# Expert weights through two rings of 11 places in one queue, and three bodies of an expert pass instead of four

## The reference, cut to what matters

```python
def swiglu(h, w1, w3, w2):
    return (jax.nn.silu(h @ w1) * (h @ w3)) @ w2

def moe_swiglu(h, router, w1, w3, w2):
    logits = (h @ router).astype(jnp.float32)
    top_v, top_i = lax.top_k(logits, TOP_K)          # TOP_K = 2 of 8
    probs = jax.nn.softmax(top_v, axis=-1)
    gate = jnp.sum(jax.nn.one_hot(top_i, N_EXPERTS, dtype=jnp.float32) * probs[..., None], axis=-2)
    out = jnp.zeros(h.shape, jnp.float32)
    for e in range(N_EXPERTS):
        out = out + gate[..., e:e + 1] * swiglu(h, w1[e], w3[e], w2[e]).astype(jnp.float32)
    return out.astype(h.dtype)
```

## Time and profile before

| What | Value |
|---|---|
| median of 3 runs | 2491.76 us |
| the profiled execution | 2489.43 us, its span 2487.6 us |
| TensorE busy (PE) | 2423.0 us, 97% |
| TensorE's weight load (PEld) | 2013.6 us, 81% |
| VectorE busy (DVE) | 1280.5 us, 51% |
| ScalarE busy (ACT) | 606.9 us, 24% |
| moved by DMA | 500.52 MB, 201 GB/s over the span |

### The profile page before, as it was taken

The page is one execution under the profiler, slowest core; times in us unless marked ns, Lnnn a source line. Parts: engine busy times, 40 slices in busy tenths (PEclk is TensorE's granted clock), DMA queues, the critical chain, the costliest instruction groups (busy, mean ns, idle before and its releaser), DMA issues. The chain is left out here.

```text
span 2487.6 us, 105448 instructions
## 1 busy us (share of the span) xinstructions
PE 2423.0 (97%) x46610; PEld 2013.6 (81%) x46610; DVE 1280.5 (51%) x3333; ACT 606.9 (24%) x1798; POOL 0.2 (0%) x4
## 2 busy tenths in 40 slices
PE   9999999999999999999999999999999999999998
PEld 7987666666699999898766666679899989888887
DVE  7666666666687676756665666668311111111111
ACT  2234333433311100223333334321111111111111
POOL 0000000000000000000000000000000000000000
PEclk9999999999999999999999999999999999999999
DMA  6334432222243443333343222234799999999997
GB/s 251 129 138 146 165 121 88 84 84 80 101 154 133 157 165 138 133 134 137 137 162 129 82 77 84 84 105 152 300 363 397 383 371 407 400 381 408 387 392 309
DMA packets 146068, 500.52 MB, mean 201 GB/s; under 512 B 18784, under 2 KB 23520, under 8 KB 143360
## 3 DMA queue, kind: packets, MB, share of 16 engines
q1 hardware_dynamic: 145792, 496.44, 53.5%
HBM read 476.08 MB, written 20.29 MB: 200 GB/s over the span
## 5 line engine op out<-in xcount | busy, mean ns | idle before, releaser
L302 PE MATMUL psum<-hT,ring 128*64 128x144 f32 (+1 forms) x4568 | 458.5, 346 | 3.4 <-DVE hT L2430 1.7
L455 PE MATMUL psum<-work,ring 128*64 128x88 f32 (+3 forms) x11264 | 417.6, 232 | 16.2 <-issue 5.8
L455 PEld LDWEIGHTS psum<-work,ring 128*64 128x64 f32 x11264 | 399.3, 136 | 35.4 <-issue 30.1
L302 PEld LDWEIGHTS psum<-hT,ring 128*64 128x64 f32 x4568 | 294.4, 137 | 95.0 <-issue 11.3
L2966 DVE TENSOR_TENSOR work<-psum,work 128x88 f32<-128x88 f32 (+3 forms) x176 | 42.4, 241 | 362.7 <-PE psum L455 362.5
L2667 PE MATMUL psum<-work,proj 128*64 128x88 f32 (+3 forms) x5632 | 203.5, 232 | 6.1 <-issue 4.5
L2667 PEld LDWEIGHTS psum<-work,proj 128*64 128x64 f32 x5632 | 196.8, 136 | 12.6 <-issue 9.6
L1776 ACT ACTIVATE work<-psum 128x256 f32<-128x256 f32 (+4 forms) x320 | 103.9, 362 | 349.9 <-PE psum L1687 84.8
L302 PE MATMUL psum<-work 128*64 128x144 f32 (+4 forms) x2096 | 155.4, 283 | 4.3 <-DVE work L1267 3.6
L302 PE MATMUL psum<-y_ret,work 128*64 128x144 f32 x2400 | 156.2, 286 | 0.8 <-DVE y_ret L532 0.8
L302 PEld LDWEIGHTS psum<-y_ret,work 128*64 128x64 f32 x2400 | 148.6, 137 | 1.0 <-issue 1.0
(11 more groups left out here) (518 smaller groups left out, 3695.7 us busy)
## 6 DMA issues: line engine op xcount, KB each, us to landing
ring<-w_ff_dram SPq DMA_DIRECT2D x424, 512.0 KB, 7.4
ring<-w_mix_dram SPq DMA_DIRECT2D x256, 512.0 KB, 3.8
proj<-w_ff_dram SPq DMA_DIRECT2D x128, 512.0 KB, 5.5
proj<-w_ff_dram SPq DMA_DIRECT2D x64, 384.0 KB, 5.8
work<-s_gla_dram SPq DMA_DIRECT2D x8, 1024.0 KB, 4.9
gla_s_out<-work SPq DMA_DIRECT2D x8, 1024.0 KB, 4.7
work<-s_ret_dram SPq DMA_DIRECT2D x8, 512.0 KB, 5.1
ret_s_out<-work SPq DMA_DIRECT2D x8, 512.0 KB, 2.7
```

What stands on the lines that cost most here:

```text
L302: last = nc.tensor.matmul(out[64 * c:64 * c + 64], weights[:, 64 * c:64 * c + 64], x, start=start, stop=stop)
L455: mm = nc.tensor.matmul(out[64 * c:64 * c + 64], ring[:, s, k, 64 * c:64 * c + 64], rhs[:, k0 + k, :], start=(k0 + k == 0), stop=(k0 + k = ...
```

## The change

The number of slots by rank becomes 88, 88, 80, 80, 80, 80, 72, 72: one class of four passes of 80 takes the place of 80, 80, 76, 76, and the bodies are three.

The weights get two rings of 11 places, for up and for down slabs. They use buffers that are free during the experts: up slabs lie in `lora_w` (2), `hT` (2), `y_ret` (2) and places 0 to 4 of `ring`; down slabs in `proj` (6), places 5 to 7 of `ring` and `merged` (2). Down weights are packed without gaps into 22 full slabs of 512 KB, so a slab runs across the border of two output tiles; a pass has 66 slabs of one size. SP's order is all 44 up slabs and then all 22 down slabs of each pass, each waiting for the slab 11 places earlier in its ring. Nothing is fetched behind the last pass. Of the 11 down places two pairs (4 and 5, 9 and 10) share a semaphore, and TensorE waits for both slabs of such a pair ahead of the first.

The first 22 slabs of the first pass are issued in `mix_out`, as the buffers come free between the join's pairs. TensorE's loops become 4 turns of 11 up slabs and 2 turns of 4 output tiles. Six banks take turns instead of four, and one count, `up_used`, that VectorE raises by 2 for each pair of slabs, replaces the two counts by which `up` waited; slab n waits until the pair that ends at slab n - 3 or n - 4 has been multiplied.

The diff, cut to its core:

```diff
-CLASSES = ((0, 2, 88), (2, 2, 80), (4, 2, 76))
+CLASSES = ((0, 2, 88), (2, 4, 80))
+EX_RING = 11
+EX_DOWN = D // 128 * FT // KT
+EX_SLABS = UP_SLABS + EX_DOWN
+UP_TURNS, DOWN_TURNS = UP_SLABS // EX_RING, EX_DOWN // EX_RING
...
+    up_slot = (slabs_in(lora_w[:, :, :], 2) + slabs_in(hT[:, :, :], 2) + slabs_in(y_ret[:, :, :], 2)
+               + [ring[:, i] for i in range(5)])
+    down_slot = slabs_in(proj[:, :, :], 6) + [ring[:, i] for i in range(5, RING)] + slabs_in(merged[:, :, :], 2)
+    DOWN_SHARED = {4: 5, 9: 10}
...
 (mix_out, SP, layer 1)
-                for j in range(RING):
-                    load_ff_slab(sp, 1, j, j, FF0 + j - RING + 1)
+                load_group(sp, S_RW_OUT, 1, 0, 4)
+                sp.wait_ge(slab_done, join_done(0))
+                up_ahead(0, 1)
+                load_group(sp, S_RW_OUT, 1, 4)
+                sp.wait_ge(slab_done, join_done(JOIN_GATES - 1))
+                up_ahead(2, 3, 4, 5)
+                load_first_group(sp, S_OUT)
+                sp.wait_ge(slab_done, join_done(OUT0 - 1))
+                down_ahead(0, 1, 2, 3, 4, 5)
+                for q in range(OUT0, OUT0 + 3):
+                    sp.wait_ge(slab_done, join_done(q))
+                    if q < OUT0 + 2:
+                        up_ahead(6 + 2 * (q - OUT0), 7 + 2 * (q - OUT0))
+                up_ahead(10)
+                down_ahead(6)
+                sp.wait_ge(slab_done, join_done(JOIN_PAIRS - 1))
+                down_ahead(7, 8, 9, 10)
...
 (experts, SP)
             def load_up(p, e, n):
-                load_ff_slab(sp, e, n, n % RING, freed_up(p, n))
+                sp.wait_ge(slab_done, count(p, EX_SLABS, FF0 + n - EX_RING + 1 - (EX_DOWN if n < EX_RING else 0)))
+                sp.dma_start(up_slot[n % EX_RING], w_ff[e, n]).then_inc(up_in[n % EX_RING], 16)
...
             with sp.Fori(0, after_first) as i:
-                for d in range(DRING):
-                    load_down(p, e, d)
-                for n in range(RING, UP_SLABS):
-                    load_up(p, e, n)
-                load_following(i, following, 2)
-                for d in range(DRING, DOWN_SLABS):
-                    load_down(p, e, d)
+                e = sp.value_load(ctl[0:1, bass.ds(i, 1)], min_val=0, max_val=NE)
+                for n in range(UP_SLABS):
+                    load_up((i, 1), e, n)
+                for d in range(EX_DOWN):
+                    load_down((i, 1), e, d)
...
 (experts, TensorE)
+                pe.wait_ge(up_in[s], turn * 16 + count(p, UP_TURNS * 16, earlier * 16 + 16))
+                pe.wait_ge(sig("up_used"), turn * EX_RING + count(p, UP_SLABS, GRANTED + s - 3))
...
-                with pe.Fori(0, UP_SLABS // RING) as g:
-                    for n in range(RING):
-                        up(p, cap, n, g)
-                for n in range(UP_SLABS // RING * RING, UP_SLABS):
-                    up(p, cap, n, 0)
+                with pe.Fori(0, UP_TURNS) as g:
+                    for s in range(EX_RING):
+                        up(p, cap, s, g)
...
-                with pe.Fori(0, KT // 2) as t:
-                    for m in range(2):
+                with pe.Fori(0, DOWN_TURNS) as t:
+                    for m in range(0, KT // DOWN_TURNS, 2):
                         down(p, cap, t, m)
...
 (host: the packing of the down weights)
-        for c in range(3):
-            n = 6 if c == 2 else 8
-            w_ff[e, UP_SLABS + c::3, :, 0:n] = s2[:, :, 8 * c:8 * c + n]
+        w_ff[e, UP_SLABS:EX_SLABS] = s2.transpose(0, 2, 1, 3).reshape(EX_DOWN, KT, 128, 128).transpose(0, 2, 1, 3)
```

More of the change, by code:

```diff
@@ L2166, in _, with up_ahead, down_ahead @@
         def _(sp):
-            load_group(sp, S_RW_OUT, 1)
-            load_first_group(sp, S_OUT)
+            def up_ahead(*slots):
+                for s in slots:
+                    sp.dma_start(up_slot[s], w_ff[1, s]).then_inc(up_in[s], 16)
+            def down_ahead(*slots):
+                for s in slots:
+                    sp.dma_start(down_slot[s], w_ff[1, UP_SLABS + s]).then_inc(down_in[s], 16)
             if dense:
+                load_group(sp, S_RW_OUT, 1)
+                load_first_group(sp, S_OUT)
                 for j in range(FF_SLABS):
@@ L2552, in _ @@
+                sp.dma_start(down_slot[d % EX_RING], w_ff[e, UP_SLABS + d]).then_inc(down_in[d % EX_RING], 16)
+            for n in range(EX_RING, UP_SLABS):
+                load_up((0, 0), 1, n)
+            for d in range(EX_RING, EX_DOWN):
+                load_down((0, 0), 1, d)
+            sp.wait_ge(sig("ctl"), 1)
             after_first = sp.value_load(ctl[0:1, ENTRIES + 1:ENTRIES + 2], min_val=NE - 1, max_val=FIXED - 1 + MAXR)
             with sp.Fori(0, after_first) as i:
-                e = expert_of(bass.ds(i, 1))
@@ L2567, in _ @@
             sp.wait_ge(sig("stored"), 4 * 16)
-            for s in range(RING):
-                per = len(range(s, UP_SLABS, RING))
-                fill = fills_before(layer, s) + fills(len(STREAM), s) + FIXED * per + 1
-                sp.wait_ge(slab_in[s], rest * (per * 16) + fill * 16)
-                settle(sp)
         @block.tensor
@@ L2655, in scatter_matrix, with down_here @@
                 last.then_inc(sig("scatter_ps"), 1)
+            def down_here(p, s, t):
+                both = 2 if s in DOWN_SHARED else 1
+                earlier = mixed_fills(s - 1) if 6 <= s < 9 else 0
+                pe.wait_ge(down_in[s], t * (both * 16) + count(p, DOWN_TURNS * both * 16, (earlier + both) * 16))
             def down(p, cap, t, m):
-                i, done = p
-                pe.wait_ge(sig("oT"), t * 2 + count(p, KT, m + 1))
-                for c in range(3):
-                    d = 3 * m + c
-                    pe.wait_ge(down_in[d], t * 16 + (i * 64 + (done * 64 + 16)))
-                    n = 6 if c == 2 else KT
-                    for k in range(n):
-                        for h in range(2):
-                            last = mm(DOWN[m][64 * h:64 * h + 64, 0:cap], down_ring[:, d, k, 64 * h:64 * h + 64],
-                                      hid[:, KT * c + k, 0:cap], start=(KT * c + k == 0), stop=(KT * c + k == FT - 1))
-                    last.then_inc(slab_done, 1)
+                pe.wait_ge(sig("oT"), t * 4 + count(p, KT, m + 1))
+                for f in range(FT):
+                    s, k = divmod(FT * m + f, KT)
+                    if k == 0 and s not in DOWN_SHARED.values():
+                        down_here(p, s, t)
+                    for h in range(2):
+                        last = mm(DOWN[m % 2][64 * h:64 * h + 64, 0:cap], down_slot[s][:, k, 64 * h:64 * h + 64],
+                                  hid[:, f, 0:cap], start=(f == 0), stop=(f == FT - 1))
+                    if k == KT - 1:
+                        last.then_inc(slab_done, 1)
+                    elif f == FT - 1:
+                        last.then_inc(sig("down_ps"), 1)
             def add_up(p, t, m):
```

119 lines of the change are left out of this document (53 added, 66 removed).

## The result

The kernel after the change takes 2495.67 us (median of 20 runs, 2491.30 to 2507.00), the kernel before in the same session 2491.17 us (20 runs, 2488.30 to 2493.15). The ratio is 1.0025, with a 95% interval of 1.0018 to 1.0032: slightly slower. Predicted were 2465 us, with a range of 2455 to 2480 and 0.06 for slower. The profiled execution took 2494.51 us, its span 2492.7. One execution of a later kernel and one of the kernel before took 7 and 9 ms; no number here takes them in.

What follows compares the result with a forecast made beforehand. TensorE was taken to bound passes 1 and 2, the weight queue passes 3 to 8: 499.0 - 527.1 = -28.1 us, plus 1.2 in pass 1, gives -26.9, so 2465 us as median, range 2455 to 2480.

Steps and rivals of the forecast that it cites:

- 499.0 us for passes 3 to 8: Weight queue in passes 3 to 8: 1.1 + 1.4 + 492.8 + 3.7 us, never running dry, against 527.1 before.
- SP's read of the table between passes: Border between passes: SP's table read stands behind 11 issued slabs, so it costs zero.
- the lead: Slabs landed ahead of TensorE: 9.3 after pass 3, then 8.6, 7.9 and 7.2; below 11, so some always under way.
- the larger loop: Jump back of TensorE's body of 407 matmul rows: code taken as kept, 0 us, with 11.2 us as upper end.
- Rival A: Jump back in passes 2, 4, 5, 6 and 8: longer body fetched anew, 2.5 us each; 2474 us, chance 0.16.
- rival C: Same jumps back, each code packet waiting its longest, 11.2 us per pass: slower, 2517 us, chance 0.06.
- First runs: TensorE's waits when a body first runs: 1.8 us in pass 3 and 3.8 in pass 7, sum 5.6.
- Pass 1: TensorE does four slabs, not five, before waiting about 2.5 us for VectorE; pass 1.2 us longer.
- the join: Six slabs (7.7 us) enter the queue ahead of the output matrix: zero cost, from 0 to +7.7 us.
- the rotation of banks: Up slabs wait for a multiply two slabs back, not three: costed at nothing.
- the signs: Profile after: 408 to 411 GB/s in passes 4 to 8, DMA waits in 7 and 8, no code packets in repeated passes.
- Rival B: Queue in passes 3 to 8: gaps not for want of places, mean stays 391.7 GB/s; 2487 us, chance 0.12.

Runs made afterwards that it cites:

- the mended kernel: The kernel after with 32 idle counts ahead of SyncE's loop and 32 small unused TensorE products at the start of the experts: 2475.03 us, ratio 0.9941 to the kernel before.
- the 32 products: 32 unused 32x32 by 8 TensorE products at the experts' start of the kernel after: 2491.34 us alone, 2475.03 us with 32 idle counts ahead of SyncE's loop.

## Why the prediction was wrong

The prediction had 499.0 us for passes 3 to 8, and the trace has 529.9, 30.9 more. The experiments divide that, by their own traces: 517.4 us with SyncE's loop in another place (12.5 less), 508.6 with TensorE's bodies moved too (8.8 less), and 9.6 that no experiment takes away.

- **The step that failed first: "SP's read of the table between passes stands behind 11 issued slabs: zero."** The border takes 7.1 us where the loop lies badly and 1.3 where it lies well, with the same read of the table, so the time is not the table's. And the cover that I named doesn't exist. What hides a pause of SyncE is what it has issued and what has not landed; by my own account the lead is 7.2 to 9.3 of 11 places landed, so only 1.7 to 3.8 slabs are under way, 2.2 to 4.9 us at 1.28 each. The windows above show it: 340 GB/s and then 70, 4 to 8 us behind the last issue at 2020.42. In the kernel with both parts of its code moved SyncE pauses longer, 9.3 us (2114.67 to 2123.96), behind 11 slabs issued together, and the queue stays at 403 to 416 GB/s in windows of 2 us: there the 11 slabs are under way.
- **The second, on the larger loop: "I take 0, the row nearest in size."** The body of 407 matmul rows is kept in passes 2, 4, 6 and 8 and fetched again in pass 5 with 12.1 us of code waits (6.03 and 1.74 of them in the rows above), close to the upper end that I had set (11.2) and given a chance of 0.06. Rival A had the mechanism, but in each later pass and at 2.5 us; it came once, and its size was rival C's. The reason I gave against it, that the body of 329 rows is kept, is true (three bodies in the kernel before) and doesn't carry over. The same section of the Trainium skill gives TensorE 128 KiB in blocks of 16 KiB, and says that a jump to outside a window of two pages fetches. The traces disagree with the second for TensorE: in the kernel before with three bodies a body that takes five packets is kept over four passes. They would fit the first if the body of 407 rows, 6.2 to 7.4 packets long, touches one packet more or less by its place; how many it touches no run shows.
- **First runs: 5.6 us.** With both places mended they are 12.0 (3.8 in pass 3, 8.2 in pass 7). That the longer body has more to fetch, through a full queue, would explain it; no run takes the two apart.
- **The rest.** In the mended kernel TensorE's waits in passes 3 to 8 are 13.9 us and its products fill 494.7 of the 508.6, where the prediction had 5.6 and 489.6. The queue is at 410 GB/s in passes 5 and 6 and 405 in pass 7, but at 391 and 395 in passes 3 and 4. That TensorE's first run leaves the places full there, and that a stall of either side takes from the other when the rings are full or empty, so that the larger of two sums is too little, is argued. What lengthens the products by 5.1 us is open.
- **Pass 1** was expected at 1.2 us more, with the wait for VectorE after 128 products of about 2.5 us. It has this wait, 2.41 us, and takes 1.5 us more (94.25 against 92.73):

```profile
1771.24 2.68 PE L2661 MATMUL psum<-work,y_ret 128*64 128x88 f32 x64 [2.41 <-DVE work L2992]
```

- **What held.** No wait for a DMA in passes 3 to 6 in the kernel after; 410 GB/s where slabs are under way (2022 to 2024 us; passes 5 and 6 of the mended kernel); the join undisturbed as far as the spread shows (pass 1 starts at 1763.70 us after the change, at 1761.48 with the 32 products, against 1762.32); the rotation of banks and the 80 slots without a wait that shows. Of the signs, the rate of 408 to 411 through passes 4 to 8 and the quiet of passes 4 and 5 on the code queue failed, as did the wait for weights in pass 8, which the waits view does not show, though the pass takes 84.31 us where unheld products would take 77.6.
- **What the change is worth.** Of the two kernels as they stand it is a loss of 0.25%. But before's loop happens to lie well and after's badly: put 5 instructions behind a packet's border, the kernel before loses 0.88%; with both parts of its code moved, the kernel after gains 0.59%. Rival B is out for most of its price: where a mean of 391.7 GB/s should have stayed, passes 5 and 6 hold 410 and passes 3 to 7 together 402 once code no longer stalls either side.

## What to carry to other kernels

When an edit changes the length or the place of code that is jumped back over, look at the queues that carry instructions, pass by pass, before explaining its time by the work it does; a few idle instructions ahead of the loop are the test. A comparison of two kernels holds an accident of place in each, and here the accident (0.6% and 0.9%) was as large as what the change is worth without it (0.6%), or larger. And cover for a pause of the engine that issues is what is under way, not the depth of the ring.

## What the runs showed of the hardware that was not expected

- SyncE's loop is fetched again at every jump back when it ends 5 instructions behind a border of 128 in its compiled order (ends at 773 and 901, five kernels, 82 to 84 packets on q14), for some 7 us each, and not when it ends 37, 55 or 119 behind one (nine traces, 51 to 54 packets). Whether the end or the start is what counts, these places leave open. The Trainium skill ("Runtime: NRT & Kernel Launch", "Instruction fetch mechanics") speaks of blocks of 16 KiB for every engine; here q14's packets have 8 KB.
- A count of a semaphore by TensorE takes 0.139 us (17.78 us for 128; 37.35 for 256, so 0.146); on SyncE 128 of them cost nothing that shows.
- A wait for code costs a second time by the clock. With SyncE's loop kept and TensorE's not, the wait of 6.47 us before pass 5 takes the granted clock from 1.00 to 0.50, the lower level of 1.2 GHz, and 64 products take 4.54 us instead of 2.44:

```profile
2116.00:2118.00 2.00, 1.57 (x18) 0.67 (x14) 0.91 (x2) 0.70 (x4) 0.00 (x0) 1.00 1.03 410
...
2120.00:2122.00 2.00, 0.00 (x0) 0.00 (x0) 0.00 (x0) 0.00 (x0) 0.00 (x0) 0.50 1.03 397
...
2126.00:2128.00 2.00, 2.00 (x36) 2.00 (x34) 0.00 (x0) 0.24 (x1) 0.00 (x0) 0.50 0.13 27
2130.00:2132.00 2.00, 2.00 (x64) 2.00 (x62) 0.24 (x1) 0.24 (x1) 0.00 (x0) 1.00 0.78 277
```

TensorE is idle from 2117.6 to 2124.04 us; the granted clock is 0.89 from 2118 to 2120, 0.50 from 2120 to 2128 and 1.00 again from 2130. The queue falls to 27 GB/s from 2126 to 2128. TensorE freed no places while it waited, and SyncE issued nothing from 2110.19 to 2126.61 us, so a wait for code is paid by the queue as well.
